# Attention's scores and value products as three rounded products of high and low parts, in a two-layer mixer block

## What is computed

```python
# 8 query heads, 2 key/value heads, head width 128; a query block is 128 tokens
s_loc = einsum("bnqkgd,bnskd->bnkgqs", qb, kb) * scale      # windowed latent keys, |distance| <= 128
s_ctx = einsum("bnqkgd,bskd->bnkgqs", qb, k_ctx) * scale    # all context keys
p = sink_softmax(concatenate([s_loc, s_ctx]), sink_b)
out = einsum("bnkgqs,bnskd->bnqkgd", p_loc, vb) + einsum("bnkgqs,bskd->bnqkgd", p_ctx, v_ctx)
# the context tokens attend to the context only, and not at all in the last layer
```

## Time and profile before

| | |
|---|---|
| Median of 3 runs (lowest, highest) | 1292.8 us (1291.08, 1293.77) |
| The profiled execution's own time | 1292.77 us |
| Its span | 1291.0 us |
| Its mean granted TensorE clock | 0.987 |
| DMA | 236.32 MB, mean 183 GB/s |

### The profile page before, as it was taken

How to read it: one execution, slowest core, us unless ns; L and a number is a source line. 1 busy time by engine, 2 the same in 40 slices (tenths; PEclk the granted TensorE clock), 3 DMA queues, 4 the chain that set the end, 5 groups by cost and what they waited for, 6 DMA issues and landing times.

```text
span 1291.0 us, 16353 instructions
## 1 busy us (share of the span) xinstructions
PE 1231.2 (95%) x6602; PEld 955.7 (74%) x6602; DVE 773.2 (60%) x1207; ACT 536.8 (42%) x843; POOL 8.0 (1%) x10
## 2 busy tenths in 40 slices
PE   2899999999999999999999999899999999999995
PEld 0455776667677777676778888679787988889995
DVE  5344445787564565552366555585789987656554
ACT  4223444551223334344342222254665555575442
POOL 0000100000000000000000000000000000000000
PEclk9899999999999999999999999999999999999998
DMA  9999655457563343332446666512331444325541
GB/s 337 350 349 348 223 200 200 196 208 276 216 265 130 127 179 130 130 131 98 147 179 252 215 217 210 197 59 106 130 135 70 156 161 153 125 95 197 194 163 66
DMA packets 80876, 236.32 MB, mean 183 GB/s; under 512 B 9376, under 2 KB 54176, under 8 KB 59424
## 3 DMA queue, kind: packets, MB, share of 16 engines
q1 hardware_dynamic: 80800, 235.27, 51.5%
HBM read 230.54 MB, written 2.10 MB: 180 GB/s over the span
## 4 chain that ended last, share of the span: by engine, by line
PE 84%; DVE 6%; ACT 3%; SPq 3%; DMA 2%; issue 1%; DVEq 0%; ACTq 0%
PE psum_block L727 20%; PE psum_block L729 19%; PE psum_block L728 19%; PE psum_ada L600 3%; PE psum_scores L794 2%; PE psum_scores L751 2%; SPq L550 2%; PE psum_scores L772 2%; DMA raw<-in_w_ada 2%; PE psum_ada L631 2%; PE psum_scores L674 1%; PE psum_scores L676 1%; PE psum_scores L675 1%; PE psum_scores L785 1%; DVE w_lo L1171 1%
## 5 line engine op out<-in xcount | busy, mean ns | idle before, releaser
L727 PE MATMUL psum_block<-h_hi,w_hi 128*128 128x512 f32 (+1 forms) x1616 | 559.4, 346 | 2.3 <-DVE h_lo L1163 1.7
L728 PE MATMUL psum_block<-h_lo,w_hi 128*128 128x512 f32 (+1 forms) x1616 | 547.8, 339 | 0.0
L729 PE MATMUL psum_block<-h_hi,w_lo 128*128 128x512 f32 (+1 forms) x1616 | 547.7, 339 | 0.0
L1171 DVE TENSOR_TENSOR w_lo<-raw,w_hi 128x1024 fp32r<-128x1024 f32 x210 | 254.5, 1224 | 338.2 <-ACT w_hi L899 338.1
L899 ACT ACTIVATE w_hi<-raw 128x1024 fp32r<-128x1024 f32 x210 | 221.3, 1059 | 509.0 <-PE psum_block L729 472.2
L727 PEld LDWEIGHTS psum_block<-h_hi,w_hi 128*128 128x128 f32 x1616 | 306.5, 190 | 66.8 <-issue 25.1
L728 PEld LDWEIGHTS psum_block<-h_lo,w_hi 128*128 128x128 f32 x1616 | 306.7, 190 | 35.7 <-issue 3.8
L729 PEld LDWEIGHTS psum_block<-h_hi,w_lo 128*128 128x128 f32 x1616 | 306.5, 190 | 33.9
L1384 DVE SCALAR_TENSOR_TENSOR Y<-glu,small,Y 128x512 f32<-128x512 f32 (+1 forms) x240 | 130.5, 614 | 0.0
L600 PE MATMUL psum_ada<-raw,cstat 128*32 128x512 f32 x384 | 48.2, 601 | 1.0 <-DMA raw<-in_w_ada 1.0
L1014 ACT ACTIVATE T<-psum_scores,stats 128x512 f32<-128x512 f32 (+1 forms) x48 | 29.0, 618 | 48.1 <-DVE stats L1409 48.0
(11 more groups left out here) (179 smaller groups left out, 1114.7 us busy)
## 6 DMA issues: line engine op xcount, KB each, us to landing
raw<-in_w_blocks SPq DMA_DIRECT2D x105, 1024.0 KB, 4.8
raw<-in_w_ada SPq DMA_DIRECT2D x81, 1024.0 KB, 6.7
qreg<-in_w_blocks SPq DMA_DIRECT2D x8, 896.0 KB, 11.6
glu<-in_w_ada SPq DMA_DIRECT2D x5, 1024.0 KB, 11.7
kv<-in_w_ada SPq DMA_DIRECT2D x5, 1024.0 KB, 12.0
bd<-in_w_ada SPq DMA_DIRECT2D x5, 1024.0 KB, 12.0
Y<-in_xT SPq DMA_DIRECT2D x8, 512.0 KB, 7.9
T<-in_xT SPq DMA_DIRECT2D x16, 256.0 KB, 5.1
```

Of the source, the lines that this page charges most:

```text
L727: mm(ps[:, 0:n], hi, hh[:, k, t], start=(at == 0), stop=False)
L728: mm(ps[:, 0:n], hi, hl[:, k, t], start=False, stop=False)
L729: last = mm(ps[:, 0:n], lo, hh[:, k, t], start=False, stop=(at == DT - 1))
L1171: V.tensor_tensor(wl[:, u % 4, 0:n], raw_of(item)[:, cols], wh[:, u % 4, 0:n].bitcast(F32), ALU.subtract).then_inc(*C.up("lo", u))
```

## The change

The keys, values, queries and probabilities are split into a rounded high part and a low part, and every plain fp32 matmul of `scores` and `pv` becomes three fp32r matmuls (high by high, high by low, low by high).

- `both` gives a tile a second name of type fp32r at the same address.
- `split_kv`, in block 18 (`KV_SPLIT`): ACT copies the rounded `kv` into `bd`, whose LRU weights are used up by then, and DVE subtracts in place, so that `kv` keeps the low part; keys and values in two pieces of 128 x 1024.
- `split_q`, in block s: ACT between its two w_hi halves, DVE between its two w_lo halves and behind `att_out`, 128 x 512 each, into tiles 4 and 5 of `T`. ACT waits for the value products of the group before. `scores` waits for it (`q_lo`).
- `p_lo`, in block s + lag: DVE subtracts pT from the transposed probabilities in PSUM, four pieces of 128 x 512 (256 for context groups), into tiles 0 to 3 of `T`, behind `att_max` and ahead of the LRU's steps and taps. It waits for all the transposes. `pv` waits for it.
- The exponentials wait for `pv` of the group before, not only for its transposes, since `T` now holds its low parts.
- POOL zeroes `bd` again before layer 1, once the last value products of layer 0 are done, and SP loads layer 1's LRU weights four stream items of blocks later.

In the diff below, `split_kv` and `split_q` stand twice: first ACT's part, then DVE's.

```diff
+KV_SPLIT = 18
...
+        def both(name, shape):
+            base = nc.sbuf_base
+            return sb(name, shape), nc.alloc_sbuf_tensor_at(name + "_r", shape, F32R, offset=base)
...
-        T = sb("T", [P, 8, TOK])
+        T, TR = both("T", [P, 8, TOK])
...
-        kv = sb("kv", [P, KV_HEADS * TOK + 4 * KV_HEADS * HD])
-        bd = sb("bd", [P, 2, 2 * CT, P])
+        kv, kv_lo = both("kv", [P, KV_HEADS * TOK + 4 * KV_HEADS * HD])
+        bd, bd_r = both("bd", [P, 2, 2 * CT, P])
+        kv_hi = bd_r[:, :, :, :].rearrange("p g n c -> p (g n c)")
...
+        def q_group(l, s):
+            kv_head, qb, isctx = groups(l)[s]
+            t0 = (LAT if isctx else 0) + qb * QB
+            return q[:, GROUP * kv_head:GROUP * (kv_head + 1), t0:t0 + QB]
...
-                if l:
-                    sp.wait_ge(*C.at("lru_mm", l - 1, CT - 1))
-                else:
-                    sp.wait_ge(*C.at("bd_zero"))
+                sp.wait_ge(*C.at("bd_zero", l))
...
-                if item == ("w", B_OUT):
+                if item == ("w", B_OUT + 4):
                     gate_weights(1)
...
                 if l:
-                    pool.wait_ge(*C.at("scores", l - 1, max(groups(l - 1))))
+                    pool.wait_ge(*C.at("pv", l - 1, max(groups(l - 1))))
+                    nc.gpsimd.memset(bd[:, :, :, :], 0.0).then_inc(*C.up("bd_zero", l))
...
             def scores(l, s):
-                pe.wait_ge(*C.at("rope", l, "k", KV_HEADS - 1))
-                if isctx:
-                    pe.wait_ge(*C.at("evac_act", l * NB + 16 + 8 * kv + 3))
-                else:
-                    pe.wait_ge(*C.at("rope", l, "q", GROUP * kv + GROUP - 1))
+                pe.wait_ge(*C.at("kv_lo", l, 0))
+                pe.wait_ge(*C.at("q_lo", l, s))
...
+                k_hi, k_lo = (x[:, kv * TOK:(kv + 1) * TOK] for x in (kv_hi, kv_lo))
+                first = LAT if isctx else 0
                 for g in range(GROUP):
-                    qt = q[:, GROUP * kv + g, t0:t0 + QB]
-                    if isctx:
-                        last = mm(psS[:, g, LAT:TOK], qt, kT[:, kv, LAT:TOK], start=True, stop=True)
-                    else:
-                        mm(psS[:, g, :], qt, kT[:, kv, :], start=True, stop=False)
+                    q_hi, q_lo = (TR[:, 4 + i, g * QB:(g + 1) * QB] for i in range(2))
+                    ps = psS[:, g, first:TOK]
+                    mm(ps, q_hi, k_hi[:, first:TOK], start=True, stop=False)
+                    mm(ps, q_hi, k_lo[:, first:TOK], start=False, stop=False)
+                    last = mm(ps, q_lo, k_hi[:, first:TOK], start=False, stop=isctx)
+                    if not isctx:
...
             def pv(l, s):
-                pe.wait_ge(*C.at("pT", l, s, GROUP - 1))
-                pe.wait_ge(*C.at("v_out", l, KV_HEADS - 1))
+                pe.wait_ge(*C.at("p_lo", l, s, GROUP - 1))
+                pe.wait_ge(*C.at("kv_lo", l, 1))
...
-                    last = mm(psS[:, 0, :], v[:, kt, kv * HD:(kv + 1) * HD], T[:, 4 + kt, :],
-                              start=(kt == first), stop=(kt == 3))
+                    at = KV_HEADS * TOK + (kt * KV_HEADS + kv) * HD
+                    v_hi, v_lo = kv_hi[:, at:at + HD], kv_lo[:, at:at + HD]
+                    mm(psS[:, 0, :], v_hi, TR[:, 4 + kt, :], start=(kt == first), stop=False)
+                    mm(psS[:, 0, :], v_hi, TR[:, kt, :], start=False, stop=False)
+                    last = mm(psS[:, 0, :], v_lo, TR[:, 4 + kt, :], start=False, stop=(kt == 3))
...
             def att_exp(l, s):
-                    act.wait_ge(*C.at("p_tp", l, max(x for x in groups(l) if x < s), GROUP - 1))
+                    act.wait_ge(*C.at("pv", l, max(x for x in groups(l) if x < s)))
...
+            def split_kv(l):
+                act.wait_ge(*C.at("lru_mm", l, CT - 1))
+                act.wait_ge(*C.at("rope", l, "k", KV_HEADS - 1))
+                for part in range(2):
+                    w = slice(part * KV_HEADS * TOK, (part + 1) * KV_HEADS * TOK)
+                    if part:
+                        act.wait_ge(*C.at("v_out", l, KV_HEADS - 1))
+                    fn(kv_hi[:, w], kv[:, w], ACT.Copy).then_inc(*C.up("kv_hi", l, part))
+
+            def split_q(l, s):
+                kv_head, qb, isctx = groups(l)[s]
+                if s != min(groups(l)):
+                    act.wait_ge(*C.at("pv", l, max(x for x in groups(l) if x < s)))
+                else:
+                    act.wait_ge(*C.at("lru_h", l, CT - 1))
+                if isctx:
+                    act.wait_ge(*C.at("evac_act", l * NB + 16 + 8 * kv_head + 3))
+                else:
+                    act.wait_ge(*C.at("rope", l, "q", GROUP * kv_head + GROUP - 1))
+                fn(TR[:, 4, :].rearrange("p (g t) -> p g t", g=GROUP), q_group(l, s), ACT.Copy).then_inc(*C.up("q_hi", l, s))
...
+            def split_kv(l):
+                for part in range(2):
+                    w = slice(part * KV_HEADS * TOK, (part + 1) * KV_HEADS * TOK)
+                    dve.wait_ge(*C.at("kv_hi", l, part))
+                    V.tensor_tensor(kv_lo[:, w], kv[:, w], kv_hi[:, w].bitcast(F32), ALU.subtract
+                                    ).then_inc(*C.up("kv_lo", l, part))
+
+            def split_q(l, s):
+                dve.wait_ge(*C.at("q_hi", l, s))
+                V.tensor_tensor(TR[:, 5, :].rearrange("p (g t) -> p g t", g=GROUP), q_group(l, s),
+                                TR[:, 4, :].rearrange("p (g t) -> p g t", g=GROUP).bitcast(F32), ALU.subtract).then_inc(*C.up("q_lo", l, s))
+
+            def p_lo(l, s):
+                k0 = 2 if groups(l)[s][2] else 0
+                dve.wait_ge(*C.at("p_tp", l, s, GROUP - 1))
+                for g in range(GROUP):
+                    dve.wait_ge(*C.at("pT", l, s, g))
+                    V.tensor_tensor(TR[:, k0:4, g * QB:(g + 1) * QB], psS[:, g, k0 * P:TOK].rearrange("p (k q) -> p k q", q=P),
+                                    TR[:, 4 + k0:8, g * QB:(g + 1) * QB].bitcast(F32), ALU.subtract).then_inc(*C.up("p_lo", l, s, g))
...
                 if gb + 2 < GLOB and b < NB - 1:
                     lo(unit(0, gb + 2, 1))
                 evac(gb)
+                if b == KV_SPLIT:
+                    split_kv(l)
                 if b in ROPE_AT[l]:
                     rope(l, ROPE_AT[l][b])
                 if b in groups(l):
                     att_max(l, b)
+                if b - TP_LAG[l] in groups(l):
+                    p_lo(l, b - TP_LAG[l])
                 if b in LRU_MM[l]:
```

More of the change, by code:

```diff
@@ L575, in _ @@
                 if l:
-                    pool.wait_ge(*C.at("scores", l - 1, max(groups(l - 1))))
+                    pool.wait_ge(*C.at("pv", l - 1, max(groups(l - 1))))
+                    nc.gpsimd.memset(bd[:, :, :, :], 0.0).then_inc(*C.up("bd_zero", l))
                 else:
                     pool.wait_ge(*used(last_of(BD_SLOT)))
-                    nc.gpsimd.memset(bd[:, :, :, :], 0.0).then_inc(*C.up("bd_zero"))
+                    nc.gpsimd.memset(bd[:, :, :, :], 0.0).then_inc(*C.up("bd_zero", l))
                     for slot_of_q in Q_SLOTS:
@@ L765, in scores @@
                     pe.wait_ge(*C.at("lru_tanh", l, CT - 1, 1))
-                t0 = (LAT if isctx else 0) + qb * QB
+                k_hi, k_lo = (x[:, kv * TOK:(kv + 1) * TOK] for x in (kv_hi, kv_lo))
+                first = LAT if isctx else 0
                 for g in range(GROUP):
-                    qt = q[:, GROUP * kv + g, t0:t0 + QB]
-                    if isctx:
-                        last = mm(psS[:, g, LAT:TOK], qt, kT[:, kv, LAT:TOK], start=True, stop=True)
-                    else:
-                        mm(psS[:, g, :], qt, kT[:, kv, :], start=True, stop=False)
+                    q_hi, q_lo = (TR[:, 4 + i, g * QB:(g + 1) * QB] for i in range(2))
[4 more added lines that the diff above has]
+                    if not isctx:
                         far = (1 - qb) * QB
@@ L1028, in att_pT @@
                     act.wait_ge(*C.at("p_tp", l, s, g))
-                    fn(T[:, 4 + k0:8, g * QB:(g + 1) * QB],
+                    fn(TR[:, 4 + k0:8, g * QB:(g + 1) * QB],
                        psS[:, g, k0 * P:TOK].rearrange("p (k q) -> p k q", q=P), ACT.Copy).then_inc(*C.up("pT", l, s, g))
@@ L1100, in _ @@
                         y_hi(l, b)
+                    if b in groups(l):
+                        split_q(l, b)
                     if b < NB - 1:
```

## The result

The changed kernel takes 1304.2 us (median of four runs, 1302.1 to 1305.5), against 1293.0 for the kernel before on the same chips: the ratio is 1.0084, 95% interval 1.0069 to 1.0100. That is 11.2 us slower, where 10.0 were forecast, and 1.4 us above the time forecast. The profiled execution took 1304.6 us with a span of 1302.8, mean granted clock 0.98; the profile before has a span of 1291.0, so the spans differ by 11.8.

What follows compares the result with a forecast made beforehand. PE, busy 95%, was taken as the bound. From 1292.8 us: layer 0 8.6 faster, layer 1 14.6 slower (waits 20.2 less 5.6 saved), clock +4, so +10.0: 1302.8 us, range 1286 to 1312.

Steps and rivals of the forecast that it cites:

- What PE saves: Attention products on PE: three fp32r products beat one fp32 product, saving 8.6 us in layer 0 and 5.6 in layer 1.
- Layer 0 hidden: Layer 0 attention: DVE's idle time covers the added p_lo and q_lo work, so PE never waits and 8.6 us are won.
- Block 21: Layer 1, start of block 21: PE waits 0.8 us for w_lo, since kv_lo adds 2.3 to DVE in block 18.
- Scores 22: Layer 1, before the score products of group 22: PE waits 4.0 us for q_lo.
- Values 22, 25, 29, 32: Layer 1, before the value products of these four groups: PE waits 3.9, 4.4, 1.5 and 3.2 us for p_lo.
- Scores 29: Layer 1, before the score products of group 29: PE waits 2.4 us for q_lo.
- The sum of waits: Layer 1: all seven new waits of PE for DVE's results together, 20.2 us.
- The clock: PE behind layer 1's waits: three of four above 3 us drop the clock, 1.8 each, partly regained: +4 us.
- Rival 1: Both layers: all added work is hidden, no waits, 14.2 us faster, 1278.6 us; chance 12%.
- Rival 2: Layer 1: every wait over 2 us drops the clock, five falls costing 9.0: 1307.8 us, 1311.6 with slow masks; chance 15%.
- Rival 3: Layer 1: waits are half as long, 10.0 us, with one clock fall of 1.8: 1290.4 us; chance 12%.
- Rival 4: PE's products: three fp32r take as long as one fp32, so only waits and clock remain: 1317 us; chance 3%.

Runs made afterwards that it cites:

- experiment 1: The changed kernel with the split in layer 0 alone, layer 1 keeping plain fp32 products: 1285.05 us, ratio 0.9930 to the kernel before.
- experiment 7: The changed kernel with p_lo computed a second time in layer 0: 1306.41 us, ratio 1.0103 to the kernel before.
- experiment 2: The changed kernel with the split in layer 1 alone, layer 0 keeping plain fp32 products: 1315.87 us, ratio 1.0171 to the kernel before.
- experiment 3: The changed kernel without p_lo in layer 1, its product reading the high part again: 1288.38 us, ratio 0.9962 to the kernel before.
- Experiments 5 and 9: Changed kernel, layer 1: p_lo, q_lo (22, 29) before w_lo, taps earlier, kv split in block 17: 1288.87 us; the same with only values split there: 1286.55 us.
- experiment 4: The changed kernel with layer 1's p_lo, and q_lo of scores 22 and 29, ahead of the block's w_lo halves: 1292.44 us, ratio 0.9993.

## Why the prediction was right, point by point

- **What PE saves.** Layer 0: forecast 8.6, measured 8.3 in the ledger and 7.6 by experiment 1. The same stretch takes 454.75 and 454.76 us in the two traces that leave layer 0 plain, against the 446.44 to 446.47 of experiment 7, so the 8.3 is sure. A head of scores repeats after 0.81 us, not 0.79: the mask costs 0.13 between fp32r products, not the 0.11 that was taken. Right.
- **Layer 0 hidden.** Right, shown by the 2.8 us to spare, by the absence of any wait of PE there, and by experiment 7.
- **p_lo's price.** Four passes 2.47 to 2.48 us, forecast 2.46 from the earlier trace rows. Right; `q_lo` 0.68 against 0.61 as a single one.
- **Block 21, forecast 0.8.** Measured 0.2, one block later, and released by the block's gating (L1328), not by w_lo. **Scores 22, forecast 4.0.** Measured 2.67. Together 4.8 were forecast and 2.8 came. The walk carried the whole 2.3 us of `kv_lo` forward as lateness, and held DVE's idle times on the way as they were. Two of them shrank: in block 17 DVE had waited 2.10 us for the DMA of the rotation's table, and waits 0.64 after; in block 20 it had waited 0.47, and does not after. 4.8 - 1.5 - 0.5 = 2.8. The rows of these places in the timeline of DVE, before, then after:

```profile
1016.38 0.43 DVE L1318 TENSOR_TENSOR lnr<-lnr,small 128x256 f32<-128x256 f32 x1 [2.10 <-DMA lnr<-qreg]
...
1033.77 0.43 DVE L1322 TENSOR_TENSOR qreg<-qreg,lnr 128x256 f32<-128x256 f32 x1 [0.47 <-DVE qreg L1319]
```

```profile
1006.42 0.42 DVE L1359 TENSOR_TENSOR lnr<-lnr,small 128x256 f32<-128x256 f32 x1 [0.64 <-DMA lnr<-qreg]
```

  The 0.47 is the kind that added work fills. The 1.5 is not: in layer 1 nothing is added on DVE ahead of block 18. What DVE does before that wait ends 8.5 us earlier than before, much as PE's work does, but the DMA lands 10.0 us earlier. In the trace of layer 1 alone DVE waits 1.73 in that place, 1.1 more than in the changed kernel, and PE's waits up to scores 22 come to 3.6 us, 0.8 more, which fits. Scores 22 is the wait whose size was most wrong, by 1.3 us.
- **Values 22, 25, 29, 32, forecast 3.9, 4.4, 1.5, 3.2.** Measured 3.83, 4.62, 1.36 and 4.63 with the old 1.43 in it, so 3.20 new. **Scores 29, forecast 2.4.** Measured 2.4. Right to 0.2 each: both PE and DVE carry their lateness on, so the error at scores 22 did not spread.
- **The sum of waits**, forecast 20.2, is 18.3 (18.1 in the attention and the 0.2 ahead of it).
- **The clock**, forecast +4 for three falls of 1.8 with some given back. Three fell, behind the three longest waits, but they cost 1.2, 3.0 and 2.5, 6.7 in all, and nothing was given back. The term was 2.7 too small and hid the 1.9 by which the waits were too large. Outside the sum stand the +1.8 of the opening and the -1.7 of the LRU's fall, which cancel. That all this met at 1.4 us from the result is luck; the mechanism is not. Each of these errors is smaller than the 7 us allowed for the clock alone.
- **Rival 1** (all hidden) falls in layer 1 and holds in layer 0. **Rival 2** (every wait over 2 us drops the clock) falls: 2.67 and 2.41 left it alone, though experiment 2 had a fall behind the same 2.67 and experiment 3 behind the same 2.41. By the Trainium skill, TensorE: Matmul & The Clock Gate, Part 1, the throttled state is the default and activity releases it. The prediction read from this that each gap would be dearer than its length; the trace agrees behind the three longest and not behind 2.67 and 2.41. **Rival 3** (waits half as long) falls: 18.3 is nine tenths of 20.2. **Rival 4** (three products as dear as one) falls with 0.81 against 0.97.
- **What came after.** In two places the reading of the waits did not carry over to experiments. Experiment 3: I took scores 29's wait for a consequence of `p_lo`. Experiments 5 and 9: I priced each removed wait as won, and the next late thing on DVE (`q_lo` in all groups, then `att_out`) took 5.7 and 2.1 us of it back. DVE's lateness in layer 1 is one thing; the waits are only the places where it comes out.

Left open, and not tried: why the rotation's DMA landed earlier with respect to DVE in block 17 (DVE waits 0.64 or 0.65 there in seven of the experiments' traces too, all with layer 0 split), and what decides whether the clock falls behind a wait of 2 to 3 us.

## What to carry to other kernels

Work put on an engine that is busy 60% is free or dear by its place: doubled in layer 0, 14.8 us more of it cost 0.6; in layer 1, 9.8 us more cost 12.6. So walk the engine's queue at each point where the bottleneck engine will wait, stage by stage, with its slack *before* the change; and apply a change only in the stage that has slack, which here turned +11 us into -8. Where an in-order engine is late as a whole, moving one waited-for result forward hands part of the wait to the next one (3.2 of 11.4 us in experiment 4): count the excess load, not the waits. And since the falls of the clock differ between executions with the same waits, a difference of 2 us between two traces is no evidence; compare the waits.

## What the runs showed of the hardware

- **A stream of three rounded products is little cheaper than one fp32 product.** They start 0.23 us apart in a stream of 512 columns, against 0.86: 0.69 for three. The whole gain of a product is 0.17 us, and a mask of 128 columns between them takes 0.13.
- **The clock does not follow the length of the wait alone.** In the LRU step whose wait of 2.00 us was followed by the lower level before, the changed kernel waits as long and keeps 2.4 GHz (timeline of PE):

```profile
974.87 3.70 PE L763 MATMUL psum_scores<-T,bd 128*128 128x512 f32 x8 [1.99 <-DVE T L1383]
```

  Eight products in 3.70 us, where the earlier trace rows has 5.40. The LRU step before this one waits 2.8 us in each of the twelve traces: three keep the clock behind it (before, changed, experiment 4), nine lose it. Layer 0 alone:

```profile
920.80 5.19 PE L764 MATMUL psum_scores<-T,bd 128*128 128x512 f32 x8 [2.82 <-DVE T L1403]
```

  In the attention, 2.67 us before scores 22 left it alone in the changed kernel and dropped it in experiment 2, 2.41 before scores 29 dropped it in experiment 3, and 1.92 before scores 25 in experiment 4. Those of 3.8 us and over dropped it in every trace.
- **A fall can cost more than the 1.8 us of the earlier trace rows** when it comes at the value products of layer 1: 1.2, 3.0 and 2.5. The records behind values 25 start 0.43 apart instead of 0.23 for the whole group (timeline of PE):

```profile
1089.01 0.63 PE L808 MATMUL psum_scores<-T_r,bd_r 128*128 128x512 f32 x1
1089.43 0.63 PE L809 MATMUL psum_scores<-T_r,kv_r 128*128 128x512 f32 x1
...
1093.27 0.63 PE L809 MATMUL psum_scores<-T_r,kv_r 128*128 128x512 f32 x1
```
